# Opening the dilated attention stage inside the last projection products, and scoring two of its three groups in rounded passes

## What is computed

```python
DIL_CONFIGS = ((128, 1), (512, 4), (2048, 16))          # window, stride d
def band_attend(q, k, v, d, nw):                         # one group
    # rows are regrouped by residue mod d; 128-query blocks see [previous block, own block]
    s = jnp.einsum('brnqhe,brnkhe->brnhqk', qb, kk)      # 4 heads of 128
    s = jnp.where(valid, s, NEG)
    m = jnp.max(s, axis=-1, keepdims=True)
    p = jnp.exp(s - m)
    l = jnp.sum(p, axis=-1, keepdims=True)
    o = jnp.einsum('brnhqk,brnkhe->brnqhe', p / l, vv)
```

## Time and profile before

| | us |
|---|---|
| median of 3 runs | 2821.64 (2819.12 to 2824.57) |
| the profiled execution's own time | 2820.37 |
| its span, first to last instruction | 2818.2 |
| PE busy in the span | 2759.3 (98%) |
| DVE, ACT and POOL busy | 1758.5, 1113.7 and 364.9 |
| start of product N - 4 (PE) | 2276.36 |
| scores of tile 0 | 2299.46 |
| scores of tile 46, the first turn without transposes | 2496.14 |

### The profile page before, as it was taken

The page is one execution under the profiler, slowest core; times in us unless marked ns, Lnnn a source line. Parts: engine busy times, 40 slices in busy tenths (PEclk is TensorE's granted clock), DMA queues, the critical chain, the costliest instruction groups (busy, mean ns, idle before and its releaser), DMA issues.

```text
span 2818.2 us, 38685 instructions
## 1 busy us (share of the span) xinstructions
PE 2759.3 (98%) x13662; PEld 2278.4 (81%) x13662; DVE 1758.5 (62%) x3819; ACT 1113.7 (40%) x3357; POOL 364.9 (13%) x574
## 2 busy tenths in 40 slices
PE   7999999999999999999999999999999989989999
PEld 6787888888787888888787888788888779988887
DVE  5486666768678633325575767776765656557664
ACT  5433131222326224215434453532323348756532
POOL 0001010100101000000001132313324022210000
PEclk9999999999999999999999999999999999999999
DMA  4276555555676634324266676868777788647642
GB/s 169 86 239 199 190 186 175 183 181 176 199 244 205 202 106 145 99 99 150 94 250 229 224 245 226 286 219 286 262 267 246 253 283 286 215 151 244 200 142 95
DMA packets 282873, 559.16 MB, mean 198 GB/s; under 512 B 31168, under 2 KB 81920, under 8 KB 282680
## 3 DMA queue, kind: packets, MB, share of 16 engines
q1 hardware_dynamic: 248440, 453.89, 49.5%
q0 software_dynamic: 34240, 102.80, 10.0%
HBM read 423.85 MB, written 132.72 MB: 197 GB/s over the span
## 4 chain that ended last, share of the span: by engine, by line
PE 93%; DVE 3%; DMA 2%; ACT 1%; issue 1%; SPq 0%; DVEq 0%; ACTq 0%
PE ps L130 26%; PE ps L132 25%; PE ps L131 25%; PE ps L3560 2%; PE ps L3532 2%; PE ps L3081 2%; PE ps L3065 1%; PE ps L3569 1%; PE ps L3119 1%; PE ps L237 1%; PE ps L2122 1%; PE ps L2390 1%; PE ps L3548 1%; PE ps L3543 1%; DMA tok_b_dram<-shared_o 1%; PE ps L1149 1%
## 5 line engine op out<-in xcount | busy, mean ns | idle before, releaser
L130 PE MATMUL ps<-b_wp,b_sring 128*128 128x512 f32 x640 | 250.3, 391 | 4.4 <-DMA b_sring<-sums_dram 3.7
L131 PE MATMUL ps<-b_wp,b_sring 128*128 128x512 f32 x640 | 249.8, 390 | 0.0
L132 PE MATMUL ps<-b_wp,b_sring 128*128 128x512 f32 x640 | 249.7, 390 | 0.0
L130 PE MATMUL ps<-a_sring,a_wp 128*128 128x512 f32 x512 | 199.5, 390 | 2.6 <-DMA a_sring<-sums_a_dram 2.6
L132 PE MATMUL ps<-a_sring,a_wp 128*128 128x512 f32 x512 | 199.3, 389 | 0.0
L131 PE MATMUL ps<-a_sring,a_wp 128*128 128x512 f32 x512 | 199.2, 389 | 0.0
L132 PE MATMUL ps<-b_wp,b_xtlo 128*128 128x512 f32 x480 | 186.8, 389 | 0.0
L131 PE MATMUL ps<-b_wp,b_xthi 128*128 128x512 f32 x480 | 186.8, 389 | 0.0
L130 PE MATMUL ps<-b_wp,b_xthi 128*128 128x512 f32 x480 | 186.8, 389 | 0.0
L960 DVE TENSOR_TENSOR shared_o<-ps,b_spare 128x512 f32<-128x512 f32 x160 | 109.7, 685 | 100.5 <-PE ps L132 83.1
L802 ACT ACTIVATE ps<-shared_o 128x128 f32<-128x128 f32 (+1 forms) x408 | 108.0, 265 | 154.7 <-DVE shared_o L960 146.9
(11 more groups left out here) (461 smaller groups left out, 6823.5 us busy)
## 6 DMA issues: line engine op xcount, KB each, us to landing
b_sring<-sums_dram SPq DMA_DIRECT2D x160, 512.0 KB, 5.1
a_sring<-sums_a_dram SPq DMA_DIRECT2D x128, 512.0 KB, 5.0
b_raws<-w_b_dram SPq DMA_DIRECT2D x176, 256.0 KB, 4.3
a_raws<-w_a_dram SPq DMA_DIRECT2D x140, 256.0 KB, 4.4
kv_dram<-shared_o POOLq DMA_DIRECT2D x96, 256.0 KB, 4.2
tok_b_dram<-shared_o POOLq DMA_DIRECT2D x96, 256.0 KB, 4.5
front<-tok_b_dram SPq DMA_DIRECT2D x96, 256.0 KB, 3.7
front<-grp_dram SPq DMA_DIRECT2D x48, 260.0 KB, 4.3
```

What stands on the lines that cost most here:

```text
L130: pe.matmul(acc, a_hi, b_hi, start=first, stop=False)
L131: pe.matmul(acc, a_hi, b_lo, start=False, stop=False)
L132: return pe.matmul(acc, a_lo, b_hi, start=False, stop=last)
```

## The change

1. The first turns of the dilated stage move into the last four products. A new class `Opening` holds the buffers and operations. PE transposes tile 0 ahead of product N - 4, the memory keys ahead of N - 3, and tile 1 ahead of N - 2, into banks 6 and 7. ACT and DVE make the copies at the same places. SP loads tile 0, then the memory keys, then tiles 1 to 3, and the values of tile 0; the other values wait until all products are made. POOL builds the masks eight products before the end.
2. DVE's wait for the landed outputs goes.
3. The samples' product of round 6 moves from ahead of the last product to ahead of the one before, in each pair. DVE finishes the output of N - 2 ahead of the adding for N - 1.
4. ACT takes one exponential of a small operand ahead of its loop, so that the table of exponentials is loaded there.
5. For tiles 16 to 47, queries and keys are split into rounded high and low parts, and the scores are three passes (`split3`) instead of the product of plain operands. ACT makes both high parts after the exponentials; DVE makes both low parts from PSUM and the high parts.
6. The loads of the output stage's second tile wait for the last scores. PE waits for all outputs at turn 3 in place of turn 2.

```diff
@@ shared_stage, scalar @@
+                if n == N - 4:
+                    opening.copy_query(act, 0)
+                if n == N - 3:
+                    for m in range(MT):
+                        opening.memory_high(act, m)
+                if n == N - 2:
+                    opening.copy_query(act, 1)
...
@@ shared_stage, vector @@
-                at_once = n < N and out_of(n) is not None and kinds[out_of(n)] == "copy"
+                at_once = n == N - 1 or n < N and out_of(n) is not None and kinds[out_of(n)] == "copy"
...
@@ shared_stage, tensor @@
-                if p == (TP - 1 if f else TP - 3) and f in (0, 1, 5, 6):
+                if f in SAMPLED and p == SAMPLED[f]:
                     sample(j, f)
+                if n == N - 4:
+                    opening.turn(pe, 0)
+                if n == N - 3:
+                    opening.turn_memory(pe)
+                if n == N - 2:
+                    opening.turn(pe, 1)
                 product(n)
...
@@ class Opening @@
+    def turn(self, pe, s):
+        u, ident = s % self.U, self.core.ident
+        pe.wait_ge(self.qk_in[u], 32 * (s // self.U + 1))
+        if s == 1:
+            pe.wait_ge(self.mem_low, MT)
+        if s:
+            pe.wait_ge(self.q_copied, s)
...
+        if s:
+            pe.wait_ge(self.k_copied, s)
...
+    def high_query(self, act, s):
+        act.wait_ge(self.turned, s + 1)
+        act.activation(self.qt_hi[:, s % 2, :], self.query_bank(s), ACT.Copy).then_inc(self.q_high, 1)
...
+    def low_query(self, dve, s):
+        dve.wait_ge(self.q_high, s - NT + 1)
+        dve.tensor_tensor(self.qt_lo[:, s % 2, :], self.query_bank(s), self.qt_hi[:, s % 2, :], ALU.subtract
+                          ).then_inc(self.q_copied, 1)
+
+    def low_keys(self, dve, s):
+        at = s % self.R
+        dve.wait_ge(self.k_high, s - NT + 1)
...
@@ dil_stage, sync @@
+            opening.load(sp, 0)
+            opening.load_memory(sp)
+            for s in range(1, U):
+                opening.load(sp, s)
+            load_values(0)
+            sp.wait_ge(*tail.made(NT // 2))
...
@@ dil_stage, scalar @@
+            act.activation(front.stat[:, 0, 0:1], ident[:, 0:1], ACT.Exp)
             for s in range(TILES + 2):
...
                 if real(s - 2):
                     exps(s - 2, 0)
                     exps(s - 2, 1)
-                if real(s):
-                    copy_query(s)
...
+                if s > 2 and real(s):
+                    if opening.parted(s):
+                        opening.high_query(act, s)
+                        opening.high_keys(act, s)
+                    else:
+                        opening.copy_query(act, s)
@@ dil_stage, vector @@
-            for sem, count in tail.stored(tail.outputs[1]):
-                dve.wait_ge(sem, count)
...
                 if real(s - 2):
                     minima(s - 2, 0)
                     minima(s - 2, 1)
...
+                if s >= 2 and real(s):
+                    if opening.parted(s):
+                        opening.low_query(dve, s)
+                        opening.low_keys(dve, s)
+                    else:
+                        opening.copy_keys(dve, s)
@@ dil_stage, tensor @@
-                    m = pe.matmul(scores[:, h, 0:n, :], qt[:, s % 2, cols], kt[:, h, at, :], start=True, stop=True)
+                    if opening.parted(s):
+                        m = split3(pe, scores[:, h, 0:n, :], opening.qt_hi[:, s % 2, cols], opening.qt_lo[:, s % 2, cols],
+                                   opening.kt_hi[:, h, at, :], opening.kt_lo[:, h, at, :], True, True)
+                    else:
+                        m = pe.matmul(scores[:, h, 0:n, :], qt[:, s % 2, cols], kt[:, h, at, :], start=True, stop=True)
```

More of the change, by code:

```diff
@@ L503, in __init__, with shared_stage @@
         self.wh1, self.wl1 = prep.buffers(stack)
-def shared_stage(core, block, lead, prep, first, pairs, ops, bufs, xt_hi, xt_lo, xs_hl, spare, w_out, keys):
+def shared_stage(core, block, stack, lead, prep, first, pairs, ops, bufs, xt_hi, xt_lo, xs_hl, spare, w_out, keys, opening):
     nc, ps, io = core.nc, core.ps, core.io
@@ L770, in _ @@
                     core.recycle(lead.sems)
+                    opening.open(stack)
             for n in range(N + 2):
                 j, f, p = where(n)
+                if n == N - TP:
+                    pool.wait_ge(keys.reduced, keys.UNITS)
+                    opening.build_masks(pool)
                 if f == 0 and p in D_AT and n < N:
@@ L1111, in _ @@
                 phase = j * F + f + 1
-                at_once = n < N and out_of(n) is not None and kinds[out_of(n)] == "copy"
+                at_once = n == N - 1 or n < N and out_of(n) is not None and kinds[out_of(n)] == "copy"
+                if n == N - 4:
+                    opening.copy_keys(dve, 0)
+                if n == N - 3:
+                    for m in range(MT):
+                        opening.memory_low(dve, m)
+                if n == N - 2:
+                    opening.copy_keys(dve, 1)
                 if at_once:
@@ L3215, in out_stage, with dil_stage @@
                     stored=lambda t: (y_out[t % 2], 16 * (t // 2 + 1)) if t < NT else (dec.y_out, 16))
-def dil_stage(core, block, tail, q_src, kv_src, dst, front, ahead, mem_kv, ops_out):
+def dil_stage(core, block, tail, opening, dst, ahead, mem_v, ops_out):
     nc, ps, ident = core.nc, core.ps, core.ident
-    U, V, R = 4, 8, 3
+    front, place, rows = opening.front, opening.place, opening.rows
+    U, V, R = opening.U, opening.V, opening.R
     GROUPS = len(DIL)
     TILES = NT * GROUPS
[L3227 to L3234, removed]
+    kv_src, dst = opening.kv_src, dst[::-1]
@@ L3343, in _ @@
         def _(pool):
-            pool.wait_ge(*tail.keys)
-            pool.memset(masks[:, :], 0.0).then_inc(zeroed, 1)
-            pool.wait_ge(zeroed, 1)
-            for at, sign in ((0, -1), (1, 1), (2, -1)):
-                cols = masks[:, at * P:(at + 1) * P]
-                pool.affine_select(out=cols, in_=cols, compare_op=ALU.is_ge, fill=NEG, base=0,
-                                   pattern=[[-sign, P]], channel_multiplier=sign).then_inc(masked, 1)
             for s in range(TILES):
@@ L3397, in _ @@
                     exps(s - 2, 1)
-                if real(s):
-                    copy_query(s)
-                if s == 2:
-                    for m in range(MT):
-                        memory_high(m)
+                if s > 2 and real(s):
[3 more added lines that the diff above has]
+                    else:
+                        opening.copy_query(act, s)
             act.wait_ge(front.qturned, 1)
@@ L3559, in sums @@
                     for i, key in enumerate(order(s)):
-                        m = pe.matmul(sums_at(s)[:, h, :], pt[:, h, i, :], v_b[:, key % V, cols], start=(i == 0),
+                        m = pe.matmul(sums_at(s)[:, h, :], pt[:, h, i, :], v_at[key % V][:, cols], start=(i == 0),
                                       stop=(i == len(order(s)) - 1))
@@ L3571, in turn_probs @@
                         t.then_inc(pturned, 1)
[L3572 to L3580 removed]
+            for s in range(2, TILES + 2):
                 if s == 2:
[L3582 removed]
+                    for bank in range(3):
+                        pe.wait_ge(*tail.bank_free(bank))
                 if real(s - 2):
@@ L3585, in _ @@
                 if real(s):
-                    turn(s)
-                if s == 2:
-                    turn_memory()
+                    opening.turn(pe, s)
                 if s == TILES + 1:
@@ L3597, in _ @@
                 if s == 3:
-                    pe.wait_ge(mem_low, MT)
+                    pe.wait_ge(*tail.outputs)
                 if real(s - 3):
@@ L3656, in build @@
             keys.scores(st)
+            with ExitStack() as early:
+                opening = Opening(core, early, [io["tok_b"][g][0:T, :] for g in range(len(DIL))],
+                                  [io["kv"][g][0:T, :] for g in range(len(DIL))], mem_kv(1, 0), ops)
             with ExitStack() as ws:
```

246 lines of the change are left out of this document (148 added, 98 removed).

## The result

The changed kernel takes 2833.3 us (median of 6 runs, 2830.2 to 2837.7), the kernel before 2820.6 in 6 runs beside it: ratio 1.0043, 95% interval 1.0034 to 1.0053, that is 12 us slower. 2835 was forecast.

What follows compares the result with a forecast made beforehand. PE work was taken to bound the kernel. Rounded scores +9.9 and the opening +3.4 (-10.6 + 7.7 + 3.0 + 3.3) gave +13.3 us on 2820.37, 2833.7; with 1.3 for the median, 2835, range 2823 to 2844.

Steps and rivals of the forecast that it cites:

- The ring: Turns 16 to 47: closed path through DVE's minima, ACT's exponentials and high parts, DVE's low parts; 5.27 us with two key blocks.
- The four periods: Time once round the ring by key blocks of tiles s - 2 and s - 3: 4.29, 4.99, 4.57, 5.27 us.
- a short wait of PE in every turn: Sign expected in the changed profile's third group, with score-to-score time near 5.27 us.
- What PE gets back at the end: After turns 16 to 47: PE ahead relative to DVE and a shorter last score; 0.6 us, between nothing and 0.9.
- The wait for tile 0: Ahead of product N - 4: PE idle for most of 7.7 us until tile 0's keys land.
- Half clock in the opening: Clock falls in the wait among the last products, as in the old boundary pause; costs 3.0 us.
- Waits behind the last product: Scores of tiles 0 and 1 and turn of tile 4: 1.4, 1.8 and 0.9 us idle, together 4.1.
- The rest: 0: Output stage's second-tile loads queue on SP until the last score, behind which also the last stores stand; cost 0.
- The sum: Whole change: +9.9 us for the rounded scores, +3.4 for the moved opening, together +13.3 us.
- the ring doesn't bind: Rival, turns 16 to 47: ACT and DVE need under 4.98 us, PE keeps its 7.6 us gain; 2817 us, chance 0.12.
- the loads come in time: Rival, opening: tile 0 lands before PE wants it, the 7.7 and 3.0 us don't arise; 2824 us, chance 0.08.
- the clock falls inside the ring: Rival, turns 16 to 18 and after: PE's pauses bring half pace, +6 to +9 us; 2843 us, chance 0.11.

Runs made afterwards that it cites:

- the second one of the same kernel: Also called the second profile: the changed kernel, nothing altered, run again beside the kernel before; ratio 1.0057 (1.0043 to 1.0070).
- the 13 profiles: Profiles of the kernel before, the changed kernel (run twice) and its follow-up variants; ratios to the kernel before from 0.9957 to 1.0066.

## Why the prediction was right, point by point

- **The ring: right, and its size to 1%.** The four periods were forecast at 4.29, 4.99, 4.57 and 5.27 us and measured, minima to minima, at 4.25, 4.95, 4.52 and 5.21. The first term, minima to exponentials, was 0.06 too long (0.80 instead of 0.86: the row that I took for its start is a memset at 2455.21, and the first operation of the minima starts 0.04 later, at 2455.25); the others held to 0.02. 161.5 us were forecast for the round trips, 159.7 measured.
- **What the profile would show: one sign was wrong.** I expected a short wait of PE in every turn. For the ring the list of waits has only 4.9 us in 9 places for PE (the line of that list, then the stretch from 2455 to 2515, columns as above):

```profile
PE ps L2680 <- DVE dil_qtlo L2713: 4.9, 9, 1.0
```
```profile
2455.00:2515.00 60.00, 59.80 (x508) 57.13 (x508) 37.93 (x153) 46.38 (x141) 11.86 (x22) 1.00 0.53 178
```

  PE counts as busy for 59.80 of 60 us while each turn is 0.25 us longer than its work, since the ends of matmuls are modelled and a quarter of a microsecond drowns in them. The ring shows in the starts and in who waits for whom on DVE and ACT, not in PE's idle time.
- **What PE gets back at the end: too small, and outside its bound.** I gave back 0.6 us, at most 0.9. The score of tile 14 is 0.79 ahead of its minima, that of tile 46 2.60 ahead: 1.8 us. PE runs further ahead of DVE at the end than at the start, and a stretch measured on PE is shorter by that. The turns cost 159.7 - 1.8 - 151.0 = 6.9 us instead of 161.5 - 0.6 - 151.0 = 9.9: of the 3.0 too many, 1.8 come from the round trips and 1.2 from this term.
- **The wait for tile 0: right.** 7.7 forecast, 7.40 measured; the load was issued 0.66 us after PE was ready for product N - 4 (0.76 forecast) and landed after 6.3 (6.6). The Trainium skill ("DMA: Bandwidth & Descriptors", Anatomy of one DMA) gives 2.0 us plus the bytes by 436 GB/s for DMAs that GpSimd issues, which makes an estimate of 2.6 us for these 256 KB. These loads are SP's, which the prediction didn't say, and they took 6.3 us with the DMA engines 85 to 106% busy in the stretches above. That the load on the engines is the reason was not tested; the trace's figure was the one to use.
- **Half clock in the opening: right in kind, the size 1.6 to 2.9.** 3.0 us were taken over from the old pause. The profile of the result shows 1.6, the second one of the same kernel 2.7. The part of the slow spell that fell into the wait costs nothing.
- **Waits behind the last product: right in sum, not each.** 4.1 forecast, 1.49 + 1.49 + 0.75 = 3.73 measured.
- **"The rest: 0": wrong.** The diff moved SP's wait for the landed outputs from tile 8 to tile 4. I looked at who needs the moved value loads and not at what else stands behind that wait in the queue, the queries and keys of tile 5. It costs 1.5 us of PE's wait in both profiles of the changed kernel, and 0.1 to 2.0 in the others with that wait.
- **The sum.** Opening: forecast -10.6 + 7.7 + 3.0 + 3.3 = +3.4; measured terms 7.40 + 1.6 + 3.73 + 1.53 against 3.89 + 3.67 + 3.0 + 0.8, +2.9, and +3.1 by the places. In the second profile they are 7.09 + 2.7 + 3.74 + 1.54, +3.7, and +3.9 by the places. Turns: +9.9 forecast, +6.9. The traces say +10 to +11 where I had +13.3, the times +12 to +16. The forecast of 2835 is closer to the measured 2833 than its terms earn, and that is luck: 3 of the 13 us between the profiles arose ahead of the opening.
- **The rivals.** That the ring doesn't bind is out: 5.21, not 4.98. That the loads come in time is out. That the clock falls inside the ring is out too; it is at 1.00 there.

## What to carry to other kernels

Before splitting an operation over two engines, write down the order of each engine's instructions in one turn and look for a closed path through them; add it up from starts to starts and compare it with the turn of the busiest engine. Busy shares of 40% and 62% said nothing here, while a path of 5.21 against 4.96 us decided the 32 turns, and putting the producer ahead of unrelated work in its queue opened it for nothing. Work pulled forward into a busy stretch pays only from the point at which its data has landed: count the wait from the issue that the queue allows, and follow every wait that the change moves within a queue to all that stands behind it.

## What was not expected of the hardware

- A rounded pass of 128 columns takes 0.112 us, one of 256 columns 0.12: with half the columns a pass is hardly shorter.
- Memsets of one column on DVE take some 15 ns each when twelve follow one another, though each is shown with 0.06 us.
- Far ahead of the change, in the first layer's last products, PE waits once for 2.4 to 3.2 us for DVE. In 7 of the 13 profiles the clock fell there, in 6 it did not, and the length of the pause alone didn't decide it: after 2.51 it fell, after 3.04 and 3.17 it didn't. In the pair shown here it fell in the changed kernel only, and the stretch up to the next stage was 3.4 us longer. The seven with the fall are on average 2.2 us later at the opening (2262.6 against 2260.4), part of the 5 us by which this stretch varies; what decides the fall stays open.
